# Sixteen relative-bias rows in DRAM, and low parts of weight slabs formed by VectorE in two linear attentions

## What is computed

```
h = h + hgrn2_mixer(rms_norm(h))       # gated linear attention, 8 heads, q | f | i | g = x @ w_in
h = h + conv_ffn(rms_norm(h))
h = h + dsa_mixer(rms_norm(h))         # top-64 sparse attention, 16 heads
h = h + conv_ffn(rms_norm(h)); h = rms_norm(h)
h = h + ffn, + even_mixer (stick-breaking attention and convolution), + ffn
h = h + ffn, + odd_mixer  (GLA, gated linear attention, 4 heads), + ffn
```

## Time and profile before

| | |
|---|---|
| median of 3 runs | 1853.4 us (1850.24 to 1862.65) |
| profiled execution | 1845.45 us, of which the span of the profile is 1843.6 us |
| mean granted clock of PE in it | 0.972 |
| PE busy | 1736.8 us (94%) |
| DVE, ACT, POOL busy | 890.0, 894.3 and 639.3 us |

### The profile page before, as it was taken

The page is one execution under the profiler, slowest core; times in us unless marked ns, Lnnn a source line. Parts: engine busy times, 40 slices in busy tenths (PEclk is TensorE's granted clock), DMA queues, the critical chain, the costliest instruction groups (busy, mean ns, idle before and its releaser), DMA issues.

```text
span 1843.6 us, 30023 instructions
## 1 busy us (share of the span) xinstructions
PE 1736.8 (94%) x12126; PEld 1597.0 (87%) x12126; DVE 890.0 (48%) x1336; ACT 894.3 (49%) x1092; POOL 639.3 (35%) x146
## 2 busy tenths in 40 slices
PE   8698999999999999999999489999999989999998
PEld 7697899989679999899989369999899979979997
DVE  2587375553637555633328935332533335534332
ACT  6222456653446565554453445444554455345453
POOL 6143223346622333233266412324232244513222
PEclk9898999999999999999999689999999999999999
DMA  8931265564034554555643114554455546325552
GB/s 279 187 117 41 92 205 194 170 206 137 24 115 160 185 179 171 173 189 175 225 146 143 46 69 154 177 198 166 154 181 201 182 128 197 101 81 195 192 184 89
DMA packets 221736, 286.07 MB, mean 155 GB/s; under 512 B 12892, under 2 KB 198995, under 8 KB 221667
## 3 DMA queue, kind: packets, MB, share of 16 engines
q1 hardware_dynamic: 216323, 276.08, 44.9%
q10 hardware_dynamic: 5344, 9.02, 2.4%
HBM read 280.88 MB, written 4.19 MB: 155 GB/s over the span
## 4 chain that ended last, share of the span: by engine, by line
PE 84%; DVE 9%; ACT 3%; DMA 2%; issue 1%; POOL 0%; ACTq 0%; DVEq 0%
PE ps L1394 25%; PE ps L1395 25%; PE ps L1396 25%; DVE arena L1313 3%; PE ps L1579 2%; PE ps L1480 2%; DMA bias_rows<-arena 2%; PE ps L1470 1%; PE ps L1693 1%; DVE h L948 1%; PE ps L1703 1%; PE ps L1714 0%; DVE xn L946 0%; ACT w_hi L491 0%; DVE xn L1103 0%
## 5 line engine op out<-in xcount | busy, mean ns | idle before, releaser
L414 POOL TENSOR_TENSOR w_lo<-raw,w_hi 128x2048 fp32r<-128x2048 f32 x133 | 624.2, 4702 | 1167.5 <-ACT w_hi L491 1167.5
L1394 PE MATMUL ps<-x_hi,w_hi 128*128 128x256 f32 x2560 | 726.7, 284 | 7.7 <-DVE w_lo L973 4.0
L1395 PE MATMUL ps<-x_lo,w_hi 128*128 128x256 f32 x2560 | 725.2, 283 | 0.0
L1396 PE MATMUL ps<-x_hi,w_lo 128*128 128x256 f32 x2560 | 725.1, 283 | 0.0
L491 ACT ACTIVATE w_hi<-raw 128x2048 fp32r<-128x2048 f32 x262 | 497.8, 1909 | 256.8 <-PE ps L1396 221.4
L1394 PEld LDWEIGHTS ps<-x_hi,w_hi 128*128 128x128 f32 x2560 | 491.2, 192 | 14.9 <-issue 5.6
L1395 PEld LDWEIGHTS ps<-x_lo,w_hi 128*128 128x128 f32 x2560 | 491.2, 192 | 2.1
L1396 PEld LDWEIGHTS ps<-x_hi,w_lo 128*128 128x128 f32 x2560 | 491.2, 192 | 0.2
L973 DVE TENSOR_TENSOR w_lo<-raw,w_hi 128x2048 fp32r<-128x2048 f32 x120 | 274.8, 2290 | 373.3 <-ACT w_hi L491 373.3
L1394 PE MATMUL ps<-w_hi,g_hi 128*128 128x512 f32 x480 | 187.5, 391 | 0.0
L1395 PE MATMUL ps<-w_lo,g_hi 128*128 128x512 f32 x480 | 187.5, 391 | 0.0
(11 more groups left out here) (176 smaller groups left out, 1531.9 us busy)
## 6 DMA issues: line engine op xcount, KB each, us to landing
raw<-in_ffn_w_in SPq DMA_DIRECT2D x88, 1024.0 KB, 5.1
raw<-in_ffn_w_up SPq DMA_DIRECT2D x44, 1024.0 KB, 5.1
raw<-in_ffn_w_out SPq DMA_DIRECT2D x44, 1024.0 KB, 4.9
raw<-in_ffn_w_down SPq DMA_DIRECT2D x22, 1024.0 KB, 4.9
raw<-in_hgrn_w_in SPq DMA_DIRECT2D x16, 1024.0 KB, 8.6
raw<-in_gla_w_in SPq DMA_DIRECT2D x12, 1024.0 KB, 5.4
raw<-in_hyb_w_in SPq DMA_DIRECT2D x10, 1024.0 KB, 5.1
raw<-in_dsa_w_in SPq DMA_DIRECT2D x6, 1024.0 KB, 5.2
```

The lines of the kernel that those rows point to most:

```text
L414: pool.tensor_tensor(w_lo[slot][:, :], raw[slot][:, :], w_hi[slot][:, :].bitcast(F32), ALU.subtract)\
L1394: pe.matmul(out_ap, a_hi, b_hi, start=start, stop=False, skip_group_check=True)
L1395: pe.matmul(out_ap, a_hi, b_lo, start=False, stop=False, skip_group_check=True)
L1396: return pe.matmul(out_ap, a_lo, b_hi, start=False, stop=stop, skip_group_check=True)
```

## The change

1. The bias rows go to DRAM 16 times instead of 128, so the transfer out of L671 moves 384 KB instead of 3 MB. The read back becomes eight transfers of 16 partitions each, 256 KB apiece. All eight are issued by ACT where the one was. POOL waits for all eight.
2. `bias_vec` moves to the second half of `xn`. DVE's wait for `bias_out` moves from ahead of the attention to the first write of `xn` near its end.
3. In both linear attentions DVE does the low parts of the gate and output slabs: one after each level (seven) and one right after `cross`. POOL skips these eight slabs.

```diff
+BIAS_ROWS = 16
-        bias_dram = nc.dram_tensor("bias_rows", (ATT_HEADS, P, DISTS), F32, kind="Internal").ap()
+        bias_dram = nc.dram_tensor("bias_rows", (ATT_HEADS, BIAS_ROWS, DISTS), F32, kind="Internal").ap()
-        bias_vec = words(15488, DISTS)
+        bias_vec = xn[:, NTB - 1, 0:DISTS]
 # GpSimd, in both places
             for s in range(RING):
-                ring.skip(s, 1)
-            low_four(2)
+                ring.skip(s, 3)
             low_ffn()
...
-            pool.wait_ge(bias_in, 16)
+            pool.wait_ge(bias_in, 16 * (P // BIAS_ROWS))
 # ScalarE
-            act.dma_start(bias_dram, bias_vec[0:ATT_HEADS, :].unsqueeze(1).broadcast_to([ATT_HEADS, P, DISTS]))\
+            act.dma_start(bias_dram, bias_vec[0:ATT_HEADS, :].unsqueeze(1).broadcast_to([ATT_HEADS, BIAS_ROWS, DISTS]))\
                 .then_inc(bias_out, 16)
...
             act.wait_ge(bias_out, 16)
             act.wait_ge(h_ready, 2 * 1)
-            act.dma_start(bias_x[:, :, :], bass.AP(bias_dram.tensor, P - 1, [[DISTS - 1, P], [P * DISTS, ATT_HEADS], [1, SEQ]]))\
-                .then_inc(bias_in, 16)
+            for p0 in range(0, P, BIAS_ROWS):
+                skewed = bass.AP(bias_dram.tensor, P - 1 - p0, [[DISTS - 1, BIAS_ROWS], [BIAS_ROWS * DISTS, ATT_HEADS], [1, SEQ]])
+                act.dma_start(bias_x[p0:p0 + BIAS_ROWS, :, :], skewed).then_inc(bias_in, 16)
             high_one(0, 3)
 # VectorE, linear_attention
                     for g in range(2):
                         masked(n, g)
                         next_level(n, g)
+                    low_one(n % RING)
...
                 dve.tensor_copy(la["cross"][:, 0:H * P], flat(4, H // 4)).then_inc(la_cross, 1)
+                low_one(3)
...
                     if tb == 0:
                         dve.wait_ge(la_silu, want(la_silu))
+                        dve.wait_ge(bias_out, 16)
...
-            dve.wait_ge(bias_out, 16)
             linear_attention(la, HG_HEADS, P, [col("hgrn_gate_norm")] * NK)
-            lows_elsewhere([2, 2, 2, 2])
```

## The result

| | before | after |
|---|---|---|
| median | 1850.5 us (16 runs beside those of after) | 1834.4 us (16 runs) |
| ratio after/before | | 0.9917 [0.989, 0.9943] |
| POOL busy (x) in the profile | 639.3 us | 562.7 us (130) |

What follows compares the result with a forecast made beforehand. The prediction took PE to bound the kernel, with 84% of the span, so only its idle or slow-clock time could be won: -16.3 - 3.4 - 0.8 + 1.5 + 3.2 + 1.5 = -14.3 us, 1839 us, range 1831 to 1848.

Steps and rivals of the forecast that it cites:

- the likeliest case: Whole kernel: a time within 1% of before, about 18.5 us, given a chance of 0.72.
- First stall and its clock: Ahead of HGRN2's levels: PE's wait for DVE's diagonal disappears, -16.3 us, and the slow clock behind it, -3.4 us.
- The rival of another wait: Ahead of the levels: another wait takes the first stall's place, keeping 5 us or more; 1844 us or more, chance 0.05.
- End of HGRN2: PE's wait for DVE's last factors goes, -3.0 us; the uncovered eighth low part costs +2.2; sum -0.8 us.
- the lower end of its range: Whole kernel: -22 us, with nothing for the reads and the end of HGRN2 losing less clock.
- Low parts inside the levels: In the attention levels: low parts of 2.2 us on DVE cost nothing, because PE is never late there.
- Issues on ACT: Norm ahead of the sparse attention: seven more read issues on the path, +3.2 us.
- clock in the norm: Norm ahead of the sparse attention: PE's longer idle time lowers its clock, +1.5 us, bounds 0 and 3.4.
- Reads beside PE: Ahead of the sparse attention: reads take 20.6 us beside PE's work, costed at nothing, up to +5 us.
- End of GLA: The eighth low part costs +2.2 us, less 0.74 us of POOL's hold on a small instruction: +1.5 us.
- The slower rival: At the read issues: ACT is held until the reads are nearly through, +9.4 us, 1863 us, chance 0.04.
- the reads come for nothing: At the norm: issues go by bytes and the clock holds, -19.0 us, 1834 us, chance 0.22.

Runs made afterwards that it cites:

- Experiment 3: Kernel before with only bias_vec moved to xn and DVE's wait moved to its first write of xn; 128 rows, one read: 1839.5 us, 0.9939.
- experiment 1: Changed kernel with the low parts back on POOL, so the bias parts alone: 1835.6 us, ratio 0.9927 against before.
- experiment 4: Changed kernel with 128 bias rows (3 MB written) and one read, low parts on DVE: 1830.7 us, ratio 0.9869 against before.
- experiment 7: Changed kernel with 34 instead of 12 idle matmuls ahead of the norm before the sparse attention: 1833.6 us, ratio 0.9896 against before.
- experiments 4 to 6: Changed kernel with 128 rows and one read (1830.7 us), with 64 rows and two reads (1830.1), or with its eight reads issued ahead of the feed-forward (1828.7).
- experiment 8: Changed kernel with the eighth low part of both linear attentions on POOL instead of on DVE behind cross: 1837.9 us, ratio 0.9911 against before.
- experiment 5: Changed kernel with 64 bias rows (1.5 MB written) and two reads of 64 partitions: 1830.1 us, ratio 0.9882 against before.

## Why the prediction was right, and which term was mis-sized

Forecast -0.8% with -14.3 us, measured -0.83% with -16.1: the likeliest case, inside 1%, with the steps as they were put. That the total came so close is in part luck: the stretches below add to -17.2, and the scatter of the feed-forward networks brings such a sum nearer to the medians or further off by 1.5 us at a time. In microseconds the forecast stood on a base that was too high: 1853.4 was the median of three executions, one of them a long one, and with 16 it is 1850.5. So 1839 was forecast and 1834.4 measured, and 2.9 us of the difference are that base.

- *First stall and its clock, -16.3 and -3.4.* Right. From the second half-level on everything is 19.4 us earlier, against 19.7; the clock's part is 3.2, since the second scores of before start at 100.30 and not at 100.46. Nothing took the place of the wait: DVE is done 2 us ahead, the margin that was reckoned. Experiment 3 shows that this rested on the other parts of the change: with the large write and with POOL's low parts, 9.3 us come back, at another line. The rival of another wait does come true where only the wait is moved. Either other part keeps it off, the small write (experiment 1) or the moved low parts (experiment 4). The prediction saw neither role: it took the low parts in the levels as free, not as a cover, and did not ask what POOL does when the gate slabs come late.
- *End of HGRN2, -0.8.* The mis-sized term. The wait of 3.0 us went and the eighth low part cost +2.2, as put. But the prediction left the following scores at their time of before, and they had run at half clock: 3.58 us against 1.95, so another 1.6. It priced the clock behind the first stall and ahead of the sparse attention, but not behind this wait; only the lower end of its range, -22 us, has less lost clock there. Later the output product came to full clock earlier than before too: its first fast product starts 3.5 us after the first of all, 6.0 us in before, which gives the last 0.9. At the add, 22.8 us are gained, 19.4 of them ahead of this stretch: the term was -3.4 and not -0.8.
- *Low parts inside the levels, nothing.* Right: DVE's line 1071 stays under 0.7 us, and no PE wait there. In the 38 us from 100.6 on, the same levels, DVE is busy 24.4 us, where 24.6 was reckoned.
- *Issues on ACT, +3.2, and clock in the norm, +1.5.* The sum was near, 4.15 measured against 4.7. So was the first term: eight issues take 3.98 us against 0.42, 3.6 more, and 3.5 of them reach the norm's end. The second was put too high: the clock was worth 0.6 (experiment 7), not 1.5. PE's turn did run at half level, but DVE and ACT set the pace.
- *Reads beside PE, nothing.* Right. They are in some 20 us after the first issue, as reckoned, and the query slab's `high` waits for PE. The Trainium skill, "SBUF — State Buffer", section "Door 1: The DMA port swizzle", has some 109 GB/s for 16 partitions. The trace agrees roughly and lies 6% above it: 116 GB/s in a stretch in which almost only these reads move data.
- *End of GLA, +1.5.* Right: 1.45.
- *The slower rival* (ACT held in the issues) did not come true: no issue took over 0.48 us. Nor did the reads come for nothing. That after's 1834.4 us is the very figure of that rival is chance, for the rival stands on the base that was 2.9 us too high. Kernels with little or none of the reads' price (experiments 4 to 6) measured 1829 to 1831 us.

## What to carry to other kernels

Ask of each wait that goes not only how long it is, but at what clock the work behind it ran: 3 us of PE standing still were followed by 1.6 us or more of lost clock in three kernels of four. An instruction that issues a transfer cost ACT 0.3 to 0.7 us here, and the size didn't order these prices; put such issues where that engine waits anyway. And before work is moved between VectorE and GpSimd, count what the one does to the other's path: at the end of HGRN2 one low part on GpSimd cost more than the same low part on VectorE, and best was a place where VectorE had nothing to do. Last, measure the parts of a change together and apart: the smaller write gains beside POOL's low parts, and costs 3.7 us once these are on DVE.

## What the runs showed of the hardware

- A low part on POOL with two SBUF inputs holds a DVE instruction that also has two SBUF inputs until it is through: 0.41 to 4.73 us (experiment 8), and four instructions, one after another, to 3.9 to 5.1 us when POOL has four in a row (experiment 3). Even an instruction on 128x4 elements was held, 0.17 to 2.16 us.
- Eight reads of 16 partitions each, over all 128 partitions together, don't run side by side at the rate of one over 128: 2 MB took some 20 us from the first issue against 8.6 us in one transfer (experiment 4), with the DMA engines at a share of 1.15 from 375 to 390 us.
- After a wait of 3.0 us ahead of HGRN2's last scores the 16 matmuls ran near the half level in before (3.58 us) and in experiments 1 and 3 (3.75 and 3.62), while in experiment 8 they ran at full clock after the same wait of 2.99 us at the same place (2.02). In the norm it was the other way about: in experiment 5 the clock held through a wait of 3.04 us, and in experiment 4 it fell after one of 2.11 (the second turn took 3.78 us in place of 2.05). So the length of the last wait alone doesn't decide; what does is not shown by these runs.
